# Scan tiles of an RWKV-7 layer laid out by token: one direction per partition half, and key and b products in one matmul

## The reference

```python
def step(s, inp):
    r_t, w_t, k_t, v_t, kk_t, a_t = inp
    sa = jnp.einsum('bhvk,bhk->bhv', s, kk_t)
    s = (s * w_t[:, :, None, :] - sa[..., None] * (kk_t * a_t)[:, :, None, :]
         + v_t[..., None] * k_t[:, :, None, :])
    return s, jnp.einsum('bhvk,bhk->bhv', s, r_t)
...
wl = p['w0'] + jnp.einsum('btdr,drc->btdc', jnp.tanh(lw), p['w2'])
decay = jnp.exp(-jnp.exp(-jax.nn.softplus(-wl) - 0.5))
a = jax.nn.sigmoid(p['a0'] + jnp.einsum('btdr,drc->btdc', la, p['a2']))
kd = kf[:, :, None, :] * (1.0 + (a - 1.0) * p['k_a'])
```

## Time and profile before

| | before |
|---|---|
| median of 3 runs | 1238.47 us (1233.29 to 1239.67) |
| the profiled execution | 1235.28 us, its span 1233.6 us |
| TensorE busy, share of the span | 1126.9 us, 91% |
| VectorE busy | 683.0 us, 55% |
| ScalarE busy | 394.3 us, 32% |
| GpSimd busy | 373.8 us, 30% |
| clock granted to TensorE, mean | 0.965 |

### The profile page before, as it was taken

The page is one execution under the profiler, slowest core; times in us unless marked ns, Lnnn a source line. Parts: engine busy times, 40 slices in busy tenths (PEclk is TensorE's granted clock), DMA queues, the critical chain, the costliest instruction groups (busy, mean ns, idle before and its releaser), DMA issues. The chain is left out here.

```text
span 1233.6 us, 36488 instructions
## 1 busy us (share of the span) xinstructions
PE 1126.9 (91%) x16691; PEld 1009.9 (82%) x16691; DVE 683.0 (55%) x937; ACT 394.3 (32%) x706; POOL 373.8 (30%) x326
## 2 busy tenths in 40 slices
PE   4869998999889999995899999999999999869997
PEld 0369887899869988975899999999999999646686
DVE  0561004948746222255677777778787877374542
ACT  3331100101113233223354344444434443253321
POOL 6161111111303222313333334334534444041110
PEclk9979998999989999997899999999999999979999
DMA  9501233211102201000000000000000000180121
GB/s 375 174 1 35 69 108 107 69 35 44 60 1 73 79 29 35 1 1 10 3 4 13 4 3 4 4 4 3 4 4 4 4 3 4 63 315 35 69 103 52
DMA packets 29974, 61.76 MB, mean 50 GB/s; under 512 B 3296, under 2 KB 21364, under 8 KB 28666
## 3 DMA queue, kind: packets, MB, share of 16 engines
q1 hardware_dynamic: 28332, 54.17, 12.7%
q10 hardware_dynamic: 1488, 5.24, 1.1%
...
## 5 line engine op out<-in xcount | busy, mean ns | idle before, releaser
L609 PE MATMUL ps<-input_rounded,weights_rounded 128*128 128x386 f32 x768 | 266.3, 347 | 10.2 <-DVE zc L779 5.2
L611 PE MATMUL ps<-input_rounded,weights_rest 128*128 128x386 f32 x768 | 262.2, 341 | 0.0
L610 PE MATMUL ps<-input_rest,weights_rounded 128*128 128x386 f32 x768 | 262.2, 341 | 0.0
L1261 POOL TENSOR_TENSOR arena<-arena,lvl 128x512 f32<-128x512 f32 x108 | 136.3, 1275 | 206.9 <-DVE arena L1340 105.9
L609 PEld LDWEIGHTS ps<-input_rounded,weights_rounded 128*128 128x128 f32 x768 | 147.0, 191 | 18.4 <-issue 12.6
L610 PEld LDWEIGHTS ps<-input_rest,weights_rounded 128*128 128x128 f32 x768 | 146.8, 191 | 0.9 <-issue 0.6
L611 PEld LDWEIGHTS ps<-input_rounded,weights_rest 128*128 128x128 f32 x768 | 146.9, 191 | 0.0
L412 POOL TENSOR_TENSOR weights_rest<-arena,weights_rounded 128x2048 fp32r<-128x2048 f32 x16 | 75.6, 4722 | 209.8 <-ACT weights_rounded L458 209.8
L1014 PE MATMUL ps<-arena 64*64 64x64 f32 x2880 | 103.2, 221 | 17.6 <-DVE arena L1358 16.4
L1014 PEld LDWEIGHTS ps<-arena 64*64 64x64 f32 x2880 | 94.0, 137 | 20.7 <-DVE arena L1358 20.7
L1006 PE MATMUL ps<-arena 64*64 64x64 f32 x2880 | 104.1, 221 | 6.2 <-issue 3.4
...
## 6 DMA issues: line engine op xcount, KB each, us to landing
...
```

What stands on the lines that cost most here:

```text
L609: pe.matmul(o, w_hi[:, k, cut], hi_of_h[:, k, cols_b], start=(k == 0), stop=False)
L610: pe.matmul(o, w_hi[:, k, cut], lo_of_h[k][:, cols_b], start=False, stop=False)
L611: last = pe.matmul(o, w_lo[:, k, cut], hi_of_h[:, k, cols_b], start=False, stop=(k == KT - 1))
L1261: pool.tensor_tensor(flat(Um[l % 3]), TA[n % 2][:, :, :, 0, :].rearrange("p d a c -> p (d a) c"), lvl[:, l, :].unsqueeze(1).to_broadcast([ ...
```

## The change

In tiles whose partitions are tokens, the partition half is now the direction d and the free index runs over 8 heads (`head`). Tiles whose partitions are channels keep the old layout. It follows:

- `gram(n, d)`: b and k of one head stand side by side and go through one matmul, 64 rows x 128 columns, with 128 moving columns. 16 a chunk, in place of 32 of 64x64. In the result `GM` the rows of b are in half d and those of k in the other half.
- `UV` holds u in half d and v in the other half, so `outputs_end` and `new_state_part` are matmuls over all 128 rows x 64 columns, 16 each a chunk. They replace the v half of `outputs_begin` and the old `outputs_end` (32), and 32 of the state.
- `transpose_keys`: 16 one-pass transposes of a 64 x 128 piece, in place of 32 matmuls with the identity (64 records).
- `lora`: reads lw and la directly, 16 matmuls of 64 rows x 128 columns and 64 moving columns, in place of 8 of 128x128x128; `stage_lora` and its four ScalarE copies go.
- The blocks of `product`, `update`, `rhs`, `solve` and `transpose_v` stay 64x64 and their number stays; in half of `rhs` and in `transpose_v` row half and column half differ, or two neighbours share the column half.
- Log-decays have two columns more per block (G = 66), so that the shifted decays are views of the same tile: one subtraction (`turn_decays`) replaces three, two exponentials replace three, the scan L1365 covers 528 elements in place of 512.
- `gather_triangle` is new on ScalarE: two copies of 64 partitions x 512 put the b triangles of both directions together for the level masks. `v_by_token` and `copy_u` become two copies each, of 64 partitions.
- `decay_state` and the k half of `over_decay` move from VectorE to GpSimd.
- The pipeline gets four stages in N + 3 = 21 steps: level 1 of a chunk is at the end of one step and levels 2 to 5 in the next; the state and outputs close in the step after.
- The four loads of the first state go straight into `S[1]`, and TensorE and ScalarE turn that state before anything else of the scan.

```diff
+        OTHER = (hi, lo)
+        G = C + 2
 
...
+        GM = [take(2, 2 * PAIRS, 2, C) for _ in range(2)]
+        KBT = [take(2, 2 * PAIRS, C) for _ in range(2)]
+        UV = [take(2, 2 * PAIRS, C) for _ in range(2)]
+        UT = take(2 * PAIRS, C)
+        Um = [take(2 * PAIRS, C) for _ in range(3)]
+        X = [take(2 * PAIRS, C) for _ in range(2)]
+        Y = [take(2 * PAIRS, C) for _ in range(2)]
...
+        LA = LS[:, 0:3:2]
+        eN = xw[:, :, :, 1:1 + C]
+        eA = LA[:, :, :, 1:1 + C]
+        eB = (LS[:, 0, :, 0:C], LS[:, 2, :, 2:G])
...
+                def lora(n):
+                    earlier(pe, q_kv, 2 * n)
+                    for which, (w, src) in enumerate(((w2s, lwT), (a2s, laT))):
+                        for a in range(PAIRS):
+                            for d, r in enumerate(HALVES):
+                                at = C * (PAIRS * which + a)
+                                last = pe.matmul(ps[:, 4 + d, at:at + C], w[r, P * a:P * a + P],
+                                                 src[r, STARTS[n][d]:STARTS[n][d] + C], start=True, stop=True)
...
+                def gram(n, d):
...
+                    for a, g in HEADS:
+                        r = HALVES[g]
+                        last = pe.matmul(ps[:, 4 + 2 * d + g, P * a:P * a + P], BK[r, d, a, :, :], QK[n % 2][r, d, a, :, :],
                                          start=True, stop=True)
+                        if a == PAIRS - 1:
+                            last.then_inc(q_g[d], 1)
...
-                def transpose_keys(n):
-                    pe.wait_ge(q_mK, 2 * (n + 1))
-                    for d in DIRS:
-                        for a in range(PAIRS):
-                            for k in range(2):
-                                for r in HALVES:
-                                    last = pe.matmul(bank2(6 + d)[r, a, k, :], BK[r, d, a, k, :], eyes[r, :], start=True, stop=True)
-                        last.then_inc(q_kt, 1)
-
...
+                        for a, g in HEADS:
+                            at = C * (PAIRS * d + a)
+                            last = pe.transpose(ps[:, 4 + g, at:at + C], BK[HALVES[g], d, a, :, :].rearrange("p s c -> p (s c)"),
+                                                eyes[HALVES[g], :])
+                    last.then_inc(q_kt, 1)
...
+                    for cross in range(2):
+                        for a in range(PAIRS):
+                            for d in DIRS:
+                                g = d ^ cross
+                                pe.matmul(ps[HALVES[d], 2 + cross, C * a:C * a + C], QK[n % 2][HALVES[g], d, a, 0, :],
+                                          state[HALVES[g], d, a, :], start=(a == 0), stop=False, skip_group_check=True)
+                    rhs_keys(n, 1).then_inc(q_r1, 1)
...
+                def rhs_keys(n, cross):
+                    for a in range(PAIRS):
+                        for d in DIRS:
+                            h = PAIRS * cross + a
+                            last = pe.matmul(ps[HALVES[d], 2 + cross, C * a:C * a + C], GM[n % 2][OTHER[d], d, h, 0, :],
+                                             UV[n % 2][OTHER[d], d, h, :], start=False, stop=(a == PAIRS - 1),
+                                             skip_group_check=True)
+                    return last
...
                 def outputs_end(n):
...
+                    for d in DIRS:
+                        for a, g in HEADS:
+                            h = head(d, g, a)
+                            last = pe.matmul(by_channel(3)[HALVES[g], d, a, :], UV[n % 2][:, d, h, :], GM[n % 2][:, d, h, 1, :],
                                              start=False, stop=((d, a) == (1, PAIRS - 1)), skip_group_check=True)
...
                 def new_state_part(n):
...
-                    for d, a in BLOCKS_OF:
-                        for r in HALVES:
-                            pe.matmul(bank(2)[r, d, a, :], KBT[n % 2][r, d, a, 0, :], UT[r, d, a, :], start=True, stop=False)
-                        for r in HALVES:
-                            last = pe.matmul(bank(2)[r, d, a, :], KBT[n % 2][r, d, a, 1, :], VT[n % 2][r, d, a, :], start=False, stop=True)
+                    for d in DIRS:
+                        for a, g in HEADS:
+                            h = head(d, g, a)
+                            last = pe.matmul(by_channel(2)[HALVES[g], d, a, :], KBT[n % 2][:, d, PAIRS * g + a, :],
+                                             UV[n % 2][:, d, h, :], start=True, stop=True)
                     last.then_inc(q_state, 1)
...
+                first_state()
+                for step in range(N + 3):
+                    n0, n1, n2, n3 = step, step - 1, step - 2, step - 3
+                    if 0 <= n2 < N:
+                        product(n2, 2)
+                    if 0 <= n3 < N:
+                        new_state_part(n3)
+                    if 0 <= n2 < N:
+                        update(n2, 2)
+                    if 0 <= n3 < N:
+                        outputs_end(n3)
+                    if 0 <= n2 < N:
+                        product(n2, 3)
+                    if 0 <= n1 < N:
+                        gram(n1, 0)
+                    if 0 <= n2 < N:
+                        update(n2, 3)
+                    if 0 <= n1 < N:
+                        gram(n1, 1)
+                        transpose_keys(n1)
+                    if 0 <= n2 < N:
+                        product(n2, 4)
+                    if 0 <= n0 < N:
+                        transpose_v(n0)
+                    if 0 <= n2 < N:
+                        update(n2, 4)
+                    if 0 <= n0 < N:
+                        lora(n0)
+                    if 0 <= n2 < N:
+                        product(n2, 5)
+                        rhs_begin(n2)
+                        update(n2, 5)
+                        rhs_end(n2)
+                    if 0 <= n1 < N:
+                        product(n1, 1)
+                    if 0 <= n2 < N:
+                        solve(n2)
+                    if 0 <= n1 < N:
+                        update(n1, 1)
+                    if n2 == PC + 2:
                         final_state()
...
+                    if 0 <= n2 < N:
+                        outputs_begin(n2)
...
-                def exps(n):
+                def inverse_decay(n):
                     act.wait_ge(q_log, n + 1)
-                    act.activation(eN, LA, ACT.Exp, scale=E_HALF / 2).then_inc(q_exp, 1)
-                    act.activation(eA, LA, ACT.Exp, scale=-E_HALF / 2).then_inc(q_exp, 1)
-                    act.activation(eB, LB, ACT.Exp, scale=-E_HALF / 2).then_inc(q_exp, 1)
+                    act.activation(eN, eA, ACT.Exp, scale=E_HALF / 2).then_inc(q_eN, 1)
+
+                def decay(n):
+                    act.wait_ge(q_eN, n + 1)
+                    act.activation(LA, LA, ACT.Exp, scale=-E_HALF / 2).then_inc(q_eA, 1)
...
+                def gather_triangle(n):
+                    earlier(act, q_um[LEVELS - 1], n)
+                    for d, r in enumerate(HALVES):
+                        act.wait_ge(q_m[d], 2 * (n + 1))
+                        act.activation(UT[r], GM[n % 2][r, d, :, 0, :], ACT.Copy).then_inc(q_tri, 1)
...
+                def keys_over_decay(n):
+                    pool.wait_ge(q_kd, 2 * (n + 1))
+                    pool.wait_ge(q_eN, n + 1)
+                    earlier(pool, q_kt, n)
+                    for d in DIRS:
+                        pool.tensor_tensor(BK[:, d, :, 1 - d, :], kd[:, d], eN[:, d], ALU.mult).then_inc(q_kN, 1)
...
+                def decay_state(n):
+                    state = S[min(n // PC, 1)]
+                    pool.wait_ge(q_sa, n + 1)
+                    pool.wait_ge(q_dend, 2 * (n + 1))
+                    pool.tensor_tensor(flat(state), flat(state),
+                                       dend[:, n % 2].rearrange("p d a -> p (d a)").unsqueeze(2).to_broadcast([P, 2 * PAIRS, C]),
+                                       ALU.mult).then_inc(q_st, 1)
+
+                for step in range(N + 3):
+                    n0, n1, n2, n3 = step, step - 1, step - 2, step - 3
+                    if 0 <= n3 < N:
+                        decay_state(n3)
+                    if 0 <= n1 < N:
+                        bonus_keys(n1)
+                    if 0 <= n2 < N:
+                        mask_level(n2, 5)
+                    if 0 <= n1 < N:
+                        mask_level(n1, 0)
+                        mask_level(n1, 3)
+                        mask_level(n1, 1)
+                        mask_level(n1, 2)
+                        mask_level(n1, 4)
+                    if 0 <= n0 < N:
+                        keys_over_decay(n0)
+                        b_keys(n0)
...
-                def split_decays(n):
+                def turn_decays(n):
                     dve.wait_ge(q_cum, n + 1)
-                    dve.tensor_tensor(LB[:, 0], LA[:, 0], xw[:, 0], ALU.subtract)
```

(5 more changed lines are left out.)

553 lines of the change are left out of this document (241 added, 312 removed).

## The result

| | before | after |
|---|---|---|
| median | 1237.43 us (1233.29 to 1239.67, 4 runs) | 1167.38 us (1164.76 to 1169.18, 4 runs) |
| the profiled execution | 1235.28 us, span 1233.6 | 1167.99 us, span 1166.3 |
| TensorE busy | 1126.9 us, 91% | 1051.2 us, 90% |
| VectorE busy | 683.0 us, 55% | 649.6 us, 56% |
| ScalarE busy | 394.3 us, 32% | 420.1 us, 36% |

The ratio is 0.9436, 95% interval 0.9404 to 0.9468: 5.6% faster. 1178 us was forecast, 10.6 us more than was measured.

The account below looks back on a forecast made before the run. TensorE's issue was taken to bound the scan's middle, the inverse's chain second. With 16 steps of 23.8 us the scan ends at 1014.5, not 1072: 1235.28 - 57.5 = 1177.8, so 1178 us, range 1148 to 1221.

Parts of the forecast that it names:

- The sum for TensorE: TensorE's matmul groups in one scan step, added up: 21.4 us, low 19.8, high 27.2.
- changes of shape: TensorE switching block shape: 0.14 us each, ten a step, at most 1.4 us, taken as 0.7.
- the high bound: TensorE's step if neighbouring blocks do not overlap: 124 ns for 64 columns, 27.2 us in all.
- rival 4: Slower: 64x128 and 128x64 blocks do not overlap with neighbours on TensorE; step 28.5 us, 1253 us; chance 0.08.
- the walk: One scan step followed through levels 2 to 5 and 1: next product at 23.1 us, 23.8 with shape changes.
- rival 1: Likeliest: a scan step of 22.8 to 24.8 us, 1162 to 1194 us; chance 0.55.
- rival 2: Everything on TensorE pairs and changes of shape are hidden: step 22 us, 1149 us; chance 0.12.
- decay_state is free on GpSimd, slack of 8 us: The state's round has 8 us of slack in a step, so decay_state on GpSimd is free on the path.
- the state's own round: In a step: add_state at 5.6 us, decay 7.1 to 8.4, rhs at 16.2.
- B: Experiments' theory: the walk through the levels with in-order queues sets the step; TensorE's time counts only where nothing covers it.
- A: Experiments' theory: TensorE's issue sets every step, each microsecond shows in full; joining b and k halved the gram products.
- Rival 3: VectorE becomes the bound, its two-SBUF-input operations waiting for GpSimd: step 25.3 to 26.5 us, 1202 to 1221 us; chance 0.20.

Follow-up runs that it names:

- the split gram: Changed kernel with b and k multiplied separately again, 32 blocks of 64x64 a chunk, neighbours visiting all four quadrants; 1166.14 us.
- both gram splits: Changed kernel with b and k multiplied separately in 64x64 blocks, four quadrants in turn (1166.14 us) or one diagonal after the other (1168.94 us).
- lora in blocks: Changed kernel with lora as 32 blocks of 64x64 over the four quadrants in place of 16 of 64x128; 1166.01 us.
- queries early: Changed kernel with the forward queries ahead of factor 2 on VectorE and the decay's exponential ahead of copy_u on ScalarE; 1157.21 us.
- the combined kernel: Changed kernel with first state turned in step 1, forward queries ahead of factor 2, lora in 64x64 blocks, v in four-quadrant order; 1146.85 us.
- state twice: Changed kernel with the 16 matmuls of new_state_part issued twice, same result; 1171.99 us.
- v twice: Changed kernel with the 16 blocks of transpose_v issued twice, same result; 1178.88 us.
- decay on VectorE: Changed kernel with decay_state moved back from GpSimd to VectorE, ahead of add_outputs; 1183.31 us.
- the last run: The combined kernel with gram split over four quadrants, rhs_begin in that order, and GpSimd's level-1 mask ahead of level 3's; 1162.71 us.

## Why the prediction was nearly right

**Right: the way, the size, and TensorE's sum.** TensorE set the step before, its matmuls shrank from 25.95 to 21.54 us busy a step, and the step followed. The sum for TensorE was 21.4 us plus 0.7; start to start it is 22.20 - 0.54 = 21.7. The terms went both ways:

| term | forecast | measured |
|---|---|---|
| two gram groups of 8 | 2.0 | 1.10 + 1.00 |
| state and outputs_end | 2.8 | 1.08 + 1.08 |
| lora | 1.4 | 1.93 |
| keys | 1.1 | 0.59 |
| v | 0.94 | 0.89 |
| rhs | 1.88 | 1.65 |
| solve and begin of the outputs | 1.88 | 2.01 |
| ten groups of the levels | 9.4 | 10.3 |
| changes of shape | 0.7 | in the rows above |

Column halves do work side by side (68 ns a matmul, not the 124 of the high bound), and rival 4 is refuted. A full-row group takes 1.08 us and the 64x64 groups beside it 1.08 instead of 0.94, and a gram group with an update behind it 1.10 for the 1.00 of the one without. That fits the 0.14 us for a change of shape at most of the ten places, but no run isolates it: product 4 takes 1.05 ahead of v, where the shape stays 64x64. The Trainium skill's page "TensorEngine Tiling (Array Packing)", section Key Properties, has a drain at every change of mode; these rows agree with it as far as they go. Its section Tiling Modes lists 64x64 as four tiles that work independently; the 61 ns a block of the split gram, for 109 on one diagonal, agree.

The prediction has its gram blocks on different PSUM banks "as in the rows". The rows were not so: before, both row halves wrote one bank. The 2.0 us did not suffer from it.

**The term that failed in size: the step, 23.8 us for 22.2.** Three of the walk's waits were too long. The queries took 761.23 - 758.84 = 2.39 us and not 3.0, with two of four pieces stretched, so TensorE waited 0.54 us after product 2 and not 1.0. From product 3 to product 4 it was 744.59 - 739.76 = 4.83 and not 5.2, from product 4 to product 5 4.95 and not 4.4, from product 5 to the next product 2 7.46 (757.00 - 749.54) and not 7.8. From product 2 to product 3 it was 4.96 for 5.7. That is 22.2 for 23.1; the 0.7 for changes of shape I had added on top, although part of it falls where the walk waits anyway. So TensorE was 97% busy in a step (21.54 of 22.20), where the forecast had 93% and named anything over 95% as a sign of being wrong: the waits on VectorE's queue that were to hold TensorE back were shorter, one of 0.54 us a step in the rows. The step lies below rival 1's 22.8 to 24.8 and close to rival 2's 22.

**The terms that failed the other way.** Step 2 began at 594.17 us and not 589: the clock in the fill was 0.60 to 0.63, not 0.72, and product 1 waited 3.3 us for its mask. From product 2 of step 2 to that of step 18 it took 364.7 us for the 383 forecast, the drain 46.2 for 42.5; from 980.27 to 1003 us, in the drain, the granted clock was 0.77. -18.3 + 5.2 + 3.7 = -9.4, close to the 9.8 us between 1177.8 and 1167.99. That the time fell into rival 1's 1162 to 1194 is luck to that extent: with the fill and the drain as forecast it would have been 1177.8 - 18.3 = 1159.5.

**The step of the reasoning that failed: decay_state is free on GpSimd, slack of 8 us.** The prediction followed only the state's own round, and not what is queued behind the decay on GpSimd. In the second half that queue is the chain shown above, and the sign that it had named, a start of the inverse that waits for the level-0 mask, is there (0.54 us). Three kernels whose work for TensorE differs by 0.15 us more to 0.8 us less a step (both gram splits, lora in blocks) have the same 22.46 to 22.48 us there; queries early, which puts `add_state` earlier, has 21.90, and so has the combined kernel, whose TensorE is busy for 0.8 us less a step (20.89 of 22.00 us for 21.70 of 22.40). That the chain and not TensorE sets those steps fits all of this; no run shortened GpSimd's part of it alone, and in the run that took the decay out of it a new collision gave back more than the gain. So how much shortening that part would give stays open.

**What the halves mean for the theories.** B came nearer. At product 2 most of TensorE's time is covered (state twice: 0.32 of 0.93 us), and in the second half another chain sets the step. In the first half, outside product 2, what is added to TensorE shows in full, as A says and B too (v twice: 0.80 of 0.85); what is taken away shows only up to some 0.3 us (gram split 0.31 of 0.35, lora in blocks 0.24 of 0.80).

**Rival 3** (VectorE, held up by GpSimd, 25.3 to 26.5) did not come, but its mechanism is real: decay on VectorE and the last run lost up to 1.25 and 0.95 us a step to it. In the order of the changed kernel the operations with both inputs in SBUF mostly meet no GpSimd work. The rival's price did not follow from its rows: five or six waits of 0.57 to 1.08 us are 2.9 to 6.5 us and not 1.5 to 2.7. The Trainium skill's page "SBUF — State Buffer", section Who interferes with whom, has the shared ports as an exclusive lock and says that an operation with two inputs in SBUF contends with GpSimd's reads; that the lock is held for the whole instruction it says of VectorE's two-port modes. The 1.73 us for 0.66 beside a mask agree with a lock, 1.07 more where the mask takes 1.27.
